# First gate and value unit of a pointwise product made side by side, with the second unit's weights split earlier into a third buffer

## The reference, cut to what matters

```python
def conformer_conv(x, w_pw1, b_pw1, w_dw, b_dw, ln_g, ln_b, w_pw2, b_pw2):
    D = x.shape[-1]
    a, gate = jnp.split(x @ w_pw1 + b_pw1, 2, axis=-1)
    h = a * jax.nn.sigmoid(gate)
    h = lax.conv_general_dilated(h, w_dw[:, None, :], ...) + b_dw     # depthwise, 31 taps
    h = jax.nn.silu(layernorm(h, ln_g, ln_b))
    return h @ w_pw2 + b_pw2

# in second_block, layer i = 1
x = x + 0.5 * swiglu_ffn(rmsnorm_2(x, norm_g[i, 0]), ...)    # the network called f = 3 below
h = rmsnorm_2(x, norm_g[i, 1])
x = x + conformer_conv(h, ...)
```

## Time and profile before

| what | value |
|---|---|
| median of 3 runs | 2817.32 us (2815.48 to 2817.88) |
| time of the profiled execution | 2815.99 us |
| its span, first to last instruction | 2814.2 us |
| TensorE busy | 2770.7 us, 98% |
| VectorE busy | 2006.8 us, 71% |
| ScalarE busy | 1158.6 us, 41% |
| granted TensorE clock, mean | 0.994 of full speed |

### The profile page before, as it was taken

How to read it: one execution, slowest core, us unless ns; L and a number is a source line. 1 busy time by engine, 2 the same in 40 slices (tenths; PEclk the granted TensorE clock), 3 DMA queues, 4 the chain that set the end, 5 groups by cost and what they waited for, 6 DMA issues and landing times.

```text
span 2814.2 us, 41586 instructions
## 1 busy us (share of the span) xinstructions
PE 2770.7 (98%) x16806; PEld 2461.7 (87%) x16806; DVE 2006.8 (71%) x2958; ACT 1158.6 (41%) x1639; POOL 62.6 (2%) x22
## 2 busy tenths in 40 slices
PE   7999999999999999999999999999999999999998
PEld 7888888888888989889898899988999888789897
DVE  4456564544668969589694797875978588669795
ACT  4333544444333424334343443332434357424342
POOL 0000011111000000000000000000000000000000
PEclk9999999999999999999999999999999999999999
DMA  7223322222533333323333233322332353123332
GB/s 223 90 79 103 108 67 86 93 78 101 170 132 100 102 104 117 108 90 105 105 105 106 70 110 105 105 96 88 103 119 90 106 192 111 60 75 105 105 106 75
DMA packets 262193, 295.39 MB, mean 105 GB/s; under 512 B 6211, under 2 KB 248019, under 8 KB 259343
## 3 DMA queue, kind: packets, MB, share of 16 engines
q1 hardware_dynamic: 257008, 281.53, 30.7%
q10 hardware_dynamic: 5022, 11.57, 1.1%
HBM read 276.30 MB, written 16.78 MB: 104 GB/s over the span
## 4 chain that ended last, share of the span: by engine, by line
PE 91%; DVE 6%; ACT 1%; issue 1%; DMA 0%; ACTq 0%; DVEq 0%; SPq 0%
PE bank L1434 14%; PE bank L1436 14%; PE bank L1435 14%; PE bank L1908 8%; PE bank L1906 8%; PE bank L1907 8%; PE bank L1734 5%; PE bank L1792 2%; PE bank L2084 1%; PE bank L1449 1%; PE bank L1451 1%; PE bank L1450 1%; PE bank L1782 1%; PE bank L1754 1%; PE bank L1462 1%
## 5 line engine op out<-in xcount | busy, mean ns | idle before, releaser
L2177 DVE TENSOR_TENSOR w_lo<-w_raw,w_hi 128x2048 fp32r<-128x2048 f32 (+2 forms) x140 | 306.3, 2190 | 135.1 <-ACT w_hi L837 131.5
L837 ACT ACTIVATE w_hi<-w_raw 128x2048 fp32r<-128x2048 f32 (+2 forms) x134 | 243.0, 1820 | 235.8 <-PE bank L1436 158.5
L1434 PE MATMUL bank<-hid_hi,w_hi 128*128 128x512 f32 x816 | 317.9, 390 | 0.0
L1435 PE MATMUL bank<-hid_lo,w_hi 128*128 128x512 f32 x816 | 317.6, 389 | 0.0
L1436 PE MATMUL bank<-hid_hi,w_lo 128*128 128x512 f32 x816 | 317.5, 389 | 0.0
L1434 PE MATMUL bank<-h_hi,w_hi 128*128 128x512 f32 x752 | 298.7, 397 | 2.8 <-DVE w_lo L2177 1.7
L1436 PE MATMUL bank<-h_hi,w_lo 128*128 128x512 f32 x752 | 292.9, 389 | 0.0
L1435 PE MATMUL bank<-h_lo,w_hi 128*128 128x512 f32 x752 | 292.8, 389 | 0.0
L1436 PEld LDWEIGHTS bank<-hid_hi,w_lo 128*128 128x128 f32 x816 | 153.2, 188 | 32.1
L1434 PEld LDWEIGHTS bank<-hid_hi,w_hi 128*128 128x128 f32 x816 | 153.2, 188 | 31.4
L1435 PEld LDWEIGHTS bank<-hid_lo,w_hi 128*128 128x128 f32 x816 | 153.2, 188 | 31.2
(11 more groups left out here) (478 smaller groups left out, 7045.8 us busy)
## 6 DMA issues: line engine op xcount, KB each, us to landing
w_raw<-in_ffn_w_in_dram SPq DMA_DIRECT2D x88, 1024.0 KB, 5.0
w_raw<-in_ffn_w_out_dram SPq DMA_DIRECT2D x32, 1024.0 KB, 5.2
w_raw<-in_w_in_dram SPq DMA_DIRECT2D x28, 1024.0 KB, 5.2
w_raw<-in_w_ffn_in_dram SPq DMA_DIRECT2D x22, 1024.0 KB, 5.0
w_raw<-in_ffn_w_out_dram SPq DMA_DIRECT2D x16, 768.0 KB, 4.5
w_raw<-in_conv_w_pw_dram SPq DMA_DIRECT2D x12, 1024.0 KB, 6.6
phase_taps<-in_conv_dw_phases_dram SPq DMA_DIRECT2D x10, 1152.0 KB, 7.5
w_raw<-in_w_ffn_down_dram SPq DMA_DIRECT2D x8, 1024.0 KB, 5.3
```

The lines of the kernel that those rows point to most:

```text
L837: nc.scalar.activation(w_hi[SLOT[u]][:, 0:n], raw[s][:, 0:n], ACT.Copy).then_inc(w_hi_ready, 1)
L1434: nc.tensor.matmul(bank[b][:, 0:n], wh, xh, start=first, stop=False)
L1435: nc.tensor.matmul(bank[b][:, 0:n], wh, xl, start=False, stop=False)
L2177: v.tensor_tensor(w_lo[slot][:, 0:n], raw[s][:, 0:n], w_hi[slot][:, 0:n].bitcast(F32), ALU.subtract).then_inc(w_lo_ready, 1)
```

## The change

Unit `U_PW1 + 1`, the first value unit, gets the third slot. Its high part is made on ScalarE at the last down column of f = 3, right after that of `U_PW1`, and its low part on VectorE in the same place, ahead of tile 6 (as for f = 0 and f = 2). They are taken out of the places after the eight activation tiles. TensorE makes the units `U_PW1` and `U_PW1 + 1` by `pair_products`; the loop over n starts at 1. The zeroing of the phase pads moves behind VectorE's wait for the value unit, since the third slot's memory overlaps these pads. With one unit fewer in turn, the units `U_PW1 + 2` and later change their slot from 0 to 1 and from 1 to 0: `NEED` of `U_PW1 + 2` is then met before the network f = 3 ends, that of `U_PW1 + 3` asks for one unit where it asked for three (`U_PW1`, `U_PW1 + 1` and `U_PW1 + 2` used before; now `U_PW1`), and from `U_PW1 + 4` on it is the same. No arithmetic is added or left out.

```diff
-IN_THIRD = {U_PW2 + 2} | {_u + 1 for _u in GATE_QUADS} | {down_unit(_f, _p, 3) for _f in range(5) for _p in range(2)}
+IN_THIRD = {U_PW1 + 1, U_PW2 + 2} | {_u + 1 for _u in GATE_QUADS} | {down_unit(_f, _p, 3) for _f in range(5) for _p in range(2)}
...
                     high_next(u)
                     if f == 1 and c >= 1:
                         keep_tokens(c - 1)
-                    if c == 3 and f in (0, 2):
-                        high(FIRST_UP[f + 1])
+                    if c == 3 and f in (0, 2, 3):
+                        high(FIRST_UP[f + 1] if f < 3 else U_PW1 + 1)
...
                     for j in range(KT):
                         act.wait_ge(conv_in, j + 1)
                         hi_part(tg[j % 2][:, :], j)
-                    high(U_PW1 + 1)
                     act.wait_ge(ph_bias_landed, 16)
...
-                    for n in range(4):
+                    pe.wait_ge(w_lo_ready, U_PW1 + 2)
+                    pair_products((SLOT[U_PW1], SLOT[U_PW1 + 1]), (h_hi, h_lo), (0, 2), lambda k: pe.wait_ge(h_ready, KT * 4 + k + 1))
+                    for n in range(1, 4):
                         u = U_PW1 + 2 * n
                         pe.wait_ge(w_lo_ready, u + 1)
-                        if n > 0:
-                            pe.wait_ge(glu_arg, 2 * n)
-                        ready = (lambda k: pe.wait_ge(h_ready, KT * 4 + k + 1)) if n == 0 else None
-                        products(SLOT[u], KT, UC, (h_hi, h_lo), (0, 1), ready=ready)
+                        pe.wait_ge(glu_arg, 2 * n)
+                        products(SLOT[u], KT, UC, (h_hi, h_lo), (0, 1))
                         pe.wait_ge(w_lo_ready, u + 2)
-                        if n > 0:
-                            pe.wait_ge(glu, 2 * n)
+                        pe.wait_ge(glu, 2 * n)
                         products(SLOT[u + 1], KT, UC, (h_hi, h_lo), (2, 3))
...
-                    if c == 3 and f in (0, 2):
-                        weight_low_of(FIRST_UP[f + 1])
+                    if c == 3 and f in (0, 2, 3):
+                        weight_low_of(FIRST_UP[f + 1] if f < 3 else U_PW1 + 1)
...
                 if f == 3:
-                    for i in range(2):
-                        v.memset(xs[i][:, :, 0:SHIFTS // 2], 0.0)
-                        ins = v.memset(xs[i][:, :, SHIFTS // 2 + PH_T:], 0.0)
-                    ins.then_inc(ph_zero, 1)
...
-                    weight_low_of(U_PW1 + 1)
                     for n in range(4):
                         weight_low_of(U_PW1 + 2 * n + 2)
                         dve.wait_ge(w_used, U_PW1 + 2 * n + 2)
+                        if n == 0:
+                            for i in range(2):
+                                v.memset(xs[i][:, :, 0:SHIFTS // 2], 0.0)
+                                ins = v.memset(xs[i][:, :, SHIFTS // 2 + PH_T:], 0.0)
+                            ins.then_inc(ph_zero, 1)
```

## The result

| | before | after |
|---|---|---|
| median of 11 runs each | 2817.32 us (2815.48 to 2821.28) | 2824.79 us (2823.05 to 2827.04) |
| profiled execution | 2815.99 us, span 2814.2 | 2824.62 us, span 2822.8 |

The ratio is 1.0028, with a 95% interval of 1.002 to 1.0036: slower by 7.5 us, where 6.7 were forecast for the median.

What follows compares the result with a forecast made beforehand. TensorE, holding 91% of the chain that ended last, was taken as the bound. 1.38 + 3.68 + 1.7 = 6.76 us on 2815.99 gave 2822.75, or 2824.0 us as a median; range 2820.9 to 2826.8.

Steps and rivals of the forecast that it cites:

- Part 1: Units 192 and 193 on TensorE: paired, they take 21.89 us, a gain of 2.23 us if unit 194 could start at once.
- Part 2: Ahead of unit 194: its split stands behind gate 192's sigmoids, TensorE stops 5.91 us, unit 194 starts 3.68 us later.
- Part 3: Last down column of f = 3: VectorE's low part of 193 ahead of tile 6 delays the sums, 1.38 us.
- Part 4: TensorE behind the stop ahead of unit 194: clock falls from 2.4 to 1.2 GHz, costing 1.7 us, bounds 0 and 3.4.
- the shorter of two falls: Fall of TensorE's clock at 1534.5 in the trace before: 3.50 us at a mean of 0.51, pricing a fall at 1.7 us.
- estimate of 0.8: Alternative clock price behind the stop ahead of unit 194: 0.8 us in the place of 1.7, making the sum 5.9.
- Part 5: Moved memsets, weight loads and new slots around units 193 to 196: all cost nothing; uncovered memsets between 0 and 4 x 0.68 us.
- The sum: Whole kernel: 1.38 + 3.68 + 1.7 = 6.76 us slower, 2824.0 us as a median, 0.24% more.
- The clock didn't hold: Rival at the stop ahead of unit 194: clock holds or falls inside it, 5.06 us slower, 2822.4 us; chance 0.27.
- 329.6: Time of an earlier clock fall on TensorE: 6.80 us ran at 0.50, pricing such a fall at 3.4 us.
- the second rival: Behind the stop ahead of unit 194: clock stays low longer, 3.4 us, 8.46 us slower in all, 2825.8 us; chance 0.13.
- The pair wins: Rival ahead of unit 194: its split is done under the pair, no wait arises, -0.85 us, 2816.5 us; chance 0.05.

Runs made afterwards that it cites:

- early split alone: Kernel before plus the early split of unit 193 into the third slot, units 192 and 193 in turn, not paired: 2817.11 us, ratio 1.0004.
- table early: Changed kernel with the sigmoid table loaded early by a one-column sigmoid nobody reads, behind the last activation tile: 2821.91 us, ratio 1.0019.
- low part behind tile 6: Changed kernel with VectorE's low part of unit 193 moved from ahead of tile 6 to behind that tile's square: 2822.64 us, ratio 1.0018.
- load held back: Changed kernel with the loads of unit 195 and three taps held on SyncE's queue until gate 192 is used: 2824.22 us, ratio 1.0024.
- split of 194 ahead: Changed kernel with ScalarE's high part of unit 194 moved ahead of the sigmoids of gate 192: 2819.29 us, ratio 1.0004.
- 13 fillers: Changed kernel with 13 unneeded constant matmuls on TensorE between the pair and unit 194: 2822.30 us, ratio 1.0021.
- 26 fillers: Changed kernel with 26 unneeded constant matmuls on TensorE between the pair and unit 194: 2828.76 us (5 runs), ratio 1.004.

## Why the prediction was right, step by step

**Part 1, the pair:** right. Forecast 20.30 us to the gate's last matmul and 21.89 for the pair; measured 2276.95 - 2256.68 = 20.27 and, where nothing stops it, 21.89. The early split alone gives 24.12 - 22.71 = 1.41 of the 2.23, so the pair as such is worth 0.8.

**Part 2, unit 194 waits behind the sigmoids:** right, and shown by moving that split and nothing else. Forecast 3.68 us later, measured 27.82 - 24.12 = 3.70. The price of the table load inside the chain was shown by loading it early.

**Part 3, the low part ahead of tile 6:** the mechanism was right and its size too where the clock held: 1.38 forecast, 1.38 to 1.39 in the three profiles with that. What the step left out is a second fall of the clock. "Together 1.38 us" was too small for the profiled execution: there A grew by 2.57, and the 1.19 above are the half clock from 2247.30 to 2250.70. Part 4 looked for a fall only at the long stop.

**Part 4, the clock behind the stop:** the forecast was 1.7 us by the shorter of two falls. It was the longer one, 6.8 us, but the first 3.1 us of it (2281.4 to 2284.5) lay in the stop, so the price was 3.58 - 1.81 = 1.8. That 1.7 came so near is luck: it is half of a fall that was half as long, and the forecast did not say how much of the fall would lie in the stop. With the table early nearly all of it lay behind the stop, and the price was 2.9. The estimate of 0.8 from the Trainium skill, page "TensorE: Matmul & The Clock Gate", section "HAM oscillation — how this bites in real kernels", was too small here; the trace decides for 1.8.

**Part 5, what costs nothing:** right. Held transfers changed nothing, and the early split without the pair has the moved memsets and new slots with no stop.

**The sum** of the profiled execution, whose span is 8.6 us longer than before: 0.25 lay ahead of the place (2239.53 - 2239.28), then come 2.57 and 3.70, and from unit 194's first matmul to the end it took 2822.8 - 2284.50 = 538.3 us, where it took 2814.2 - 2277.98 = 536.2 before: 2.1, of which 1.8 are the slow matmuls. So nothing later took the delay up, as the forecast said. The medians differ by 7.5. The forecast of 6.76 lacked the 1.19, which three of the seven profiles with that wait don't have; the sum came out near with a term missing.

**The rivals:** the clock didn't hold at the long stop in any profile that had it unfilled (after, the low part behind tile 6, the load held back, the table early). The low stretch was as long as at 329.6, as the second rival had it, but not its price. The pair wins only with the order changed, and then by less than the measurement tells.

## What to carry to other kernels

When two products are put side by side, the first ends later by almost the length of the second (here 20.27 us after the start in the place of 2265.46 - 2253.86 = 11.60, where the second takes 11.0); list what was hidden under the second and waits for the first, and what stands behind that wait in the same engine's list. Work that needs nothing from the product, here a weight split and a table load, belongs ahead of that wait. A split that moves to an earlier place needs a gap there in its engine's list: two instructions later in VectorE's list, in a wait longer than the split's 2.28 us, it cost nothing.

## What the runs showed of the hardware that was not expected

The clock fell behind a short wait. Ahead of the sums TensorE stood for 1.12 us, then came 8 small matmuls. The same wait is in seven profiles, each of another kernel: in four the clock was at half behind it (after, split of 194 ahead, 13 fillers, table early; A 17.15 to 17.20), in three it stayed full (26 fillers, load held back, early split without the pair; A 15.96 to 15.97). The same instructions cost 1.2 us more or not, from one profile to the next, and what decides it is not shown. Whether this is why the changed kernel's runs reach from 2823.05 to 2827.04 was not tried; on record is that the four longest of them (2826.19 and more) have a mean granted clock of 0.991 and the shortest 0.993, so falls of the clock, at one place or another, go with that spread.

A fall of the clock cost what lay on matmuls, not its length: 1.8 us behind the stop of the changed kernel, 2.9 behind the shorter stop with the table early.
